# Attention scores from rounded halves of K and Q, SyncE's transfers of the vectors, and an identity built by GpSimd

## The chip, the cores and the metric

One Trainium2 chip, of which one core is used. The metric is the device time of one execution in microseconds. A core has five engines, each with a queue of its own that it executes in order: TensorE (PE, with PEld for its weight loads), VectorE (DVE), ScalarE (ACT), GpSimd (POOL) and SyncE (SP, which here only starts transfers). They wait for one another by semaphores.

## The reference

A transformer block of 512 tokens by 1024: a gated feed-forward network (FFN, inner width 2816), a mixer, a second FFN, and a gated embedding. The mixer adds two branches, a latent attention with 8 heads and an mLSTM with 4 heads. All is fp32. The part that the change touches is the attention:

```python
s = (jnp.einsum('bqhd,bkhd->bhqk', qn, k_nope)
     + jnp.einsum('bqhd,bkd->bhqk', qr, k_rope))
pr = jax.nn.softmax(s.astype(jnp.float32) * scale, axis=-1).astype(v.dtype)
return jnp.einsum('bhqk,bkhd->bqhd', pr, v)
```

## The kernel before

Activations lie feature-major: 8 tiles of 128 features by 512 tokens. Nearly every product is made from rounded halves: an operand a is split into `a_hi` (rounded by ScalarE to the format fp32r, which PE takes in one pass) and `a_lo = a - a_hi` (subtracted by VectorE), and three products hi·hi, hi·lo and lo·hi are added up in a bank of PSUM (`three`, L294 to L296, and `three_tm`, L301 to L303). Weights come in 193 chunks of 128x1024 through a ring of four slots: SyncE loads `w_raw`, ScalarE writes `w_hi` (L317), VectorE `w_lo` (L324), PE uses them and frees the slot.

*The attention loop.* Before it, VectorE writes Q (all 8 heads, 128 feature rows each, `Q_done`) and K (`K_done`, L1302), and ScalarE Vm. Then 32 blocks s (a head and 128 queries) run through all three engines, each with its own written order:
- PE, iteration s: `scores(s)` (L1017), one fp32 product of a 128-column piece of Q with K[:, head, :] (two records in the trace) into bank 2 + s % 3; then four transposes of block s - 4 (L1025), on iterations 12, 20 and 28 a pair output (L1038, 8 fp32 products for two heads), and six rounded products of the attention gate (L294 to L296), which fill PE's time.
- VectorE, iteration s: reduce(s), the row maximum (L1321); `nb(s)`, its scaled negative (L1322); on 12, 20 and 28 two gate copies (`ga_out`, L1308); the reciprocal of the sum of s - 2 (L1331); on 14, 22 and 30 `oT_lo` (L1312), which waits for ScalarE's `oT_hi`; on odd s the copy of the transposes of s - 4 (L1337); on every fourth s one `w_lo` (L324); on s = 6 to 25 one convolution tap of the other branch (L1222 for the first tap of each of four tiles, L1225 for the rest).
- ScalarE, iteration s: exp(s) with its sum (L1526), which waits for `nb(s)` and for the transposes of s - 4; on even s the copy of the transposes of s - 4 (L1532); the scaling of block s - 2 by its reciprocal (L1537, `norm`); on 14, 22 and 30 `oT_hi` (L1517); on every fourth s one `w_hi` (L317).

*The opening.* ScalarE starts 13 transfers of small vectors (`vec_rows`, 96 rows, read as columns after a transpose) and two of biases before its first computation. SyncE loads the first weights, a 128x128 identity from HBM, x in five parts, and further chunks. PE multiplies something of no use while it waits (`warm`), transposes the gains of the first norm, then x tile by tile, between the first products of FFN 1 (`lead_pe`). ScalarE writes `v_hi` (L2037) and the squares of h (L2043), VectorE `v_lo` and h; GpSimd adds the squares up (L560), and PE sums the result over partitions (L423) before the last products of the lead (L579, L580, L585). `lead_pe` is shared with the mixer and the second FFN; the change puts its new lines there under `n == 0`. Then the loop of FFN 1 begins with L294, at 41.

## Time and profile before

| | us |
|---|---|
| three executions | 1217.08, 1217.12, 1220.69; median 1217.12 |
| the profiled execution | 1217.22 |
| its span, first to last instruction | 1215.4 |
| PE busy | 1204.3 (99%) |
| VectorE busy | 645.3 (53%) |
| ScalarE busy | 461.9 (38%) |
| GpSimd busy | 110.7 (9%) |
| mean granted clock of PE | 0.994 |

Times in the rows are microseconds from the start of the span. A matmul's record lasts longer than the step to the next one, since they overlap in the array: the chain's numbers are the steps. "<-" before an engine and a line names what ended an idle time.

### The profile page before, as it was taken

What the parts mean: (1) busy time and instruction counts of PE and PEld (TensorE: products, weight loads), DVE (VectorE), ACT (ScalarE), POOL (GpSimd) and SP (SyncE); (2) the same over time, 40 slices, a digit from 0 to 9 for tenths busy, and PEclk for the clock granted to TensorE, in tenths of its full rate; (3) what the DMA queues carried; (4) which work ended last, traced back from release to release, by engine and by line L of the source; (5) the groups of instructions that cost most, each with busy time, mean ns of one, the idle gap of its engine ahead of it and who ended that gap; (6) DMA issues with size and microseconds to landing.
All of it is one profiled execution on the core that took longest, in us unless ns stands there. A gap on an engine that the chain in (4) does not pass through costs nothing.

```text
span 1215.4 us, 15133 instructions
## 1 busy us (share of the span) xinstructions
PE 1204.3 (99%) x5580; PEld 978.3 (80%) x5580; DVE 645.3 (53%) x1033; ACT 461.9 (38%) x696; POOL 110.7 (9%) x92
## 2 busy tenths in 40 slices
PE   9999999999999999999999999999999999999998
PEld 7788888888888886656887888888888888888887
DVE  6544444462226797765557874674444444222585
ACT  5232223322124627566343633553233232121472
POOL 3000000000003200000112201210000000000254
PEclk9999999999999999999999999999999999999998
DMA  6333333223232341111522133233333333233211
GB/s 205 119 90 102 102 100 90 89 91 114 100 89 48 70 119 53 53 35 35 157 87 70 62 114 119 97 105 94 104 87 97 99 96 104 88 103 95 96 35 70
DMA packets 102512, 111.92 MB, mean 92 GB/s; under 512 B 15326, under 2 KB 92350, under 8 KB 102214
## 3 DMA queue, kind: packets, MB, share of 16 engines
q1 hardware_dynamic: 98016, 109.20, 29.8%
q10 hardware_dynamic: 4454, 2.16, 0.6%
q8 instruction: 26, 0.43, 0.1%
q14 instruction: 16, 0.13, 0.0%
HBM read 108.19 MB, written 3.16 MB: 92 GB/s over the span
## 4 chain that ended last, share of the span: by engine, by line
PE 91%; DVE 3%; ACT 2%; issue 2%; POOL 1%; DMA 0%; DVEq 0%; SPq 0%; ACTq 0%; POOLq 0%
PE bank L294 25%; PE bank L296 24%; PE bank L295 24%; PE bank L585 2%; PE bank L579 2%; PE bank L580 2%; PE bank L301 1%; PE bank L302 1%; PE bank L303 1%; PE bank L1038 1%; PE bank L423 1%; POOL sqacc L560 1%; PE bank L1017 1%; PE bank L1705 1%; PE bank L1148 1%
## 5 line engine op out<-in xcount | busy, mean ns | idle before, releaser
L324 DVE TENSOR_TENSOR w_lo<-w_raw,w_hi 128x1024 fp32r<-128x1024 f32 x193 | 243.0, 1265 | 351.6 <-ACT w_hi L317 348.7
L294 PE MATMUL bank<-v_hi,w_hi 128*128 128x512 f32 x904 | 357.1, 395 | 0.0
L296 PE MATMUL bank<-v_hi,w_lo 128*128 128x512 f32 x904 | 352.5, 390 | 0.0
L295 PE MATMUL bank<-v_lo,w_hi 128*128 128x512 f32 x904 | 352.1, 390 | 0.0
L317 ACT ACTIVATE w_hi<-w_raw 128x1024 fp32r<-128x1024 f32 x193 | 202.1, 1056 | 358.5 <-PE bank L296 354.9
L294 PEld LDWEIGHTS bank<-v_hi,w_hi 128*128 128x128 f32 x904 | 169.9, 188 | 37.9 <-issue 3.5
L296 PEld LDWEIGHTS bank<-v_hi,w_lo 128*128 128x128 f32 x904 | 169.8, 188 | 35.8
L295 PEld LDWEIGHTS bank<-v_lo,w_hi 128*128 128x128 f32 x904 | 170.0, 188 | 33.7
L294 PE MATMUL bank<-prod_hi,w_hi 128*128 (+1 forms) x352 | 137.2, 390 | 0.0
L296 PE MATMUL bank<-prod_hi,w_lo 128*128 (+1 forms) x352 | 137.0, 389 | 0.0
L295 PE MATMUL bank<-prod_lo,w_hi 128*128 (+1 forms) x352 | 137.0, 389 | 0.0
L295 PEld LDWEIGHTS bank<-prod_lo,w_hi 128*128 128x128 f32 x352 | 66.1, 188 | 13.7
L294 PEld LDWEIGHTS bank<-prod_hi,w_hi 128*128 128x128 f32 x352 | 66.1, 188 | 13.6
L296 PEld LDWEIGHTS bank<-prod_hi,w_lo 128*128 128x128 f32 x352 | 66.1, 188 | 13.5
L434 POOL COPY sqacc<-scratch 128x512 f32<-128x512 f32 x4 | 3.7, 924 | 729.5 <-ACT scratch L491 729.5
L776 ACT ACTIVATE prod_hi<-scratch 128x512 f32 (+1 forms) x44 | 27.0, 633 | 110.9 <-DVE scratch L736 110.9
L736 DVE TENSOR_TENSOR scratch<-bank,scratch 128x512 f32<-128x512 f32 x44 | 28.3, 685 | 65.6 <-PE bank L296 65.6
L579 PE MATMUL bank<-v_hi,w_hi 128*128 128x512 f32 x128 | 51.6, 403 | 0.7 <-ACT v_hi L2037 0.4
L580 PE MATMUL bank<-v_hi,w_lo 128*128 128x512 f32 x128 | 50.7, 396 | 0.0
L770 ACT ACTIVATE scratch<-scratch 128x512 f32<-128x512 f32 x44 | 27.1, 633 | 55.5 <-DVE scratch L724 55.5
L560 POOL TENSOR_TENSOR sqacc<-sqacc,scratch 128x512 f32<-128x512 f32 x28 | 41.1, 1466 | 23.6 <-ACT scratch L550 20.7
L585 PE MATMUL bank<-v_lo,w_hi 128*128 128x512 f32 x128 | 37.3, 396 | 0.2
(263 smaller groups left out, 1349.3 us busy)
## 6 DMA issues: line engine op xcount, KB each, us to landing
w_raw<-in_ffn_w_up SPq DMA_DIRECT2D x44, 512.0 KB, 3.7
w_raw<-in_ffn_w_down SPq DMA_DIRECT2D x44, 512.0 KB, 3.4
w_raw<-in_ffn_w_gate SPq DMA_DIRECT2D x43, 512.0 KB, 3.7
w_raw<-in_w_in SPq DMA_DIRECT2D x32, 512.0 KB, 3.7
w_raw<-in_w_out SPq DMA_DIRECT2D x8, 512.0 KB, 3.4
w_raw<-in_ple_w_gate SPq DMA_DIRECT2D x8, 512.0 KB, 3.3
Mb<-m_rows ACTq DMA_DIRECT2D x8, 256.0 KB, 4.5
w_raw<-in_w_branch_mla SPq DMA_DIRECT2D x4, 512.0 KB, 4.0
```

The costliest lines, as they stand in the source:

```text
L294: nc.tensor.matmul(o, whi, a_hi, start=start, stop=False)
L295: nc.tensor.matmul(o, whi, a_lo, start=False, stop=False)
L296: return nc.tensor.matmul(o, wlo, a_hi, start=False, stop=stop)
L317: nc.scalar.activation(w_hi[:, s, :], w_raw[:, s, :], ACT.Copy).then_inc(w_hi_done, 1)
L324: nc.vector.tensor_tensor(w_lo[:, s, :], w_raw[:, s, :], w_hi[:, s, :].bitcast(F32), ALU.subtract).then_inc(w_lo_done, 1)
L560: nc.gpsimd.tensor_tensor(sqacc[:], sqacc[:], scratch[:, m % 4, :], ALU.add).then_inc(b["h_acc"], 1)
L579: nc.tensor.matmul(o[:], whi, v_hi[:, k, :], start=(k == 0), stop=False)
L580: nc.tensor.matmul(o[:], wlo, v_hi[:, k, :], start=False, stop=False)
L585: last = nc.tensor.matmul(B[4 + 2 * (j % 2) + f][:], wv(N + j, c, c + P)[0], v_lo[:, k, :], start=False, stop=(k == KD - 1))
L736: nc.vector.tensor_tensor(scratch[:, 2 + f, :], B[(6 if first else 2) + f][:], scratch[:, f, :], ALU.mult).then_inc(prod_done, 1)
L770: nc.scalar.activation(scratch[:, f, :], scratch[:, f, :], ACT.Silu).then_inc(silu0 if first else silu_done, 1)
L776: nc.scalar.activation(o, scratch[:, 2 + f, :], ACT.Copy).then_inc(phi, 1)
```

## The change

1. *Scores.* K and Q are split like the other operands. ScalarE rounds K of a head (`K_high`, 128x512) and a block's piece of Q (`Q_high`, 128x128) into `K_hi` and `Q_hi`, rings of four; VectorE subtracts (`K_low`, `Q_low`) into the place of K and Q. `scores(s)` is three products. Heads 0 to 3 and blocks 0 to 3 are split before the loop; in iteration s both engines split block s + 4, and in iterations 9, 11, 17 and 19 heads 4 to 7 as well.
2. *Vectors.* ScalarE starts only the transfer of the first norm's gains. The others, with trig, positions and biases, are started by SyncE behind the four first weight chunks (`small_loads`). PE transposes them into bank 0 just before the sum over h, and VectorE copies them after `w_lo` of chunk 3.
3. *Identity.* GpSimd writes it with a memset and an affine select; its transfer is gone. Four of the eight warm products behind the gains go.
4. *Order of the opening.* x comes in four parts of 256 features, the first of them ahead of the second half of the first weight chunk. PE takes x tile 2 between the first two chunk steps and tile 3 behind the second. ScalarE issues the squares of h earlier.

```diff
-    X_PARTS = [(0, 1), (1, 2), (2, 4), (4, 6), (6, 8)]
+    X_PARTS = [(0, 2), (2, 4), (4, 6), (6, 8)]
...
             chunks(0, [0])
+            x_tiles(2, 3)
             chunks(1, [0])
-            x_tiles(2, 4)
+            x_tiles(3, 4)
...
+        if n == 0:
+            pe.wait_ge(consts_in, CONSTS)
+            b.wait(pe, "h_ready", KD)
+            nc.tensor.transpose(B[0][:, 0:NVEC], vec_rows[0:NVEC, :], ident[0:NVEC, 0:NVEC]).then_inc(vecs_T, 1)
         b.wait(pe, "h_acc", KD)
...
             if b == 0:
-                pe.wait_ge(ms["K_done"], hd + 1)
+                pe.wait_ge(ms["qk_split"], QK_COUNT["K", hd])
+            pe.wait_ge(ms["qk_split"], QK_COUNT["Q", s])
...
-            nc.tensor.matmul(B[2 + s % 3][:], Q[:, hd, b * P:(b + 1) * P], K[:, hd, :], start=True,
-                             stop=True).then_inc(ms["scores"], 1)
+            o, q_lo = B[2 + s % 3][:], Q_lo[:, hd, b * P:(b + 1) * P]
+            nc.tensor.matmul(o, Q_hi[:, s % 4, :], K_hi[hd % 4][:], start=True, stop=False)
+            nc.tensor.matmul(o, Q_hi[:, s % 4, :], K_lo[:, hd, :], start=False, stop=False)
+            nc.tensor.matmul(o, q_lo, K_hi[hd % 4][:], start=False, stop=True).then_inc(ms["scores"], 1)
...
+    K_STEP = {9: 4, 11: 5, 17: 6, 19: 7}
...
+    def Q_high(act, s):
+        hd, b = head_block(s)
+        act.wait_ge(ms["Q_done"], HEADS)
+        if s >= 4:
+            act.wait_ge(ms["scores"], s - 3)
+        nc.scalar.activation(Q_hi[:, s % 4, :], Q[:, hd, b * P:(b + 1) * P], ACT.Copy).then_inc(ms["qk_hi"], 1)
...
+    def Q_low(dve, s):
+        hd, b = head_block(s)
+        c = slice(b * P, (b + 1) * P)
+        dve.wait_ge(ms["qk_hi"], QK_COUNT["Q", s])
+        nc.vector.tensor_tensor(Q_lo[:, hd, c], Q[:, hd, c], Q_hi[:, s % 4, :].bitcast(F32),
+                                ALU.subtract).then_inc(ms["qk_split"], 1)
...
             if s % 4 == 1 and s >= 5:
                 lo_upto(dve, GAC + (s - 5) // 4 + 3)
+            if s + 4 < STEPS:
+                Q_low(dve, s + 4)
+            if s in K_STEP:
+                K_low(dve, K_STEP[s])
             if s >= 6 and s - 6 < 4 * CONV:
                 conv_tap(dve, s - 6)
...
             if s >= 14 and s % 8 == 6:
                 oT_high(s // 8 - 1)
+            if s + 4 < STEPS:
+                Q_high(act, s + 4)
+            if s in K_STEP:
+                K_high(act, K_STEP[s])
             if s % 4 == 0 and s >= 4:
                 hi_upto(act, GAC + (s - 4) // 4 + 3)
...
-        sp.dma_start(ident[:], const["ident"]).then_inc(ident_in, 16)
         x_part(0)
+        first_chunk_half_sp(sp, 1)
         x_part(1)
-        first_chunk_half_sp(sp, 1)
+        f1[5](sp, 0, 1)
         x_part(2)
-        f1[5](sp, 0, 1)
         x_part(3)
-        x_part(4)
...
+        f1[0](sp, 2, small_loads)
...
+        plink(pool, nc.gpsimd.memset(ident[:], 0.0))
+        nc.gpsimd.affine_select(out=ident[:], in_=ident[:], compare_op=ALU.not_equal, fill=1.0, base=0,
+                                pattern=[[-1, P]], channel_multiplier=1).then_inc(pool_made, 1)
...
         half_hi(act, 0, 1)
+        x_square(0)
         x_hi(2)
+        x_square(1)
         x_hi(3)
         half_hi(act, 1, 0)
         half_hi(act, 1, 1)
-        x_square(0)
-        x_square(1)
+        x_square(2)
+        x_square(3)
...
-        warm(8, ident[:])
+        warm(4, ident[:])
```

## Rows read from the trace of the kernel before

**Rows 1.** The page: busy time by engine, and the chain's shares by engine

```profile
PE 1204.3 (99%) x5580; PEld 978.3 (80%) x5580; DVE 645.3 (53%) x1033; ACT 461.9 (38%) x696; POOL 110.7 (9%) x92
PE 91%; DVE 3%; ACT 2%; issue 2%; POOL 1%; DMA 0%; DVEq 0%; SPq 0%; ACTq 0%; POOLq 0%
```

**Rows 2.** The chain in order of time, attention loop: start, us, what

```profile
476.86 0.86 PE bank L1017 x2
...
479.55 0.86 PE bank L1017 x2
...
491.59 3.58 PE bank L1038 x16
```

**Rows 3.** Waits from 464 to 568: us in total, times, longest

```profile
ACT Pm L1526 <- DVE small L1322: 25.9, 18, 2.3
DVE small L1321 <- PE bank L1017: 20.8, 12, 4.5
```

**Rows 4.** Timeline of VectorE, blocks 13 to 16: start, us, line, operation, idle before

```profile
499.17 1.21 DVE L324 TENSOR_TENSOR w_lo<-w_raw,w_hi 128x1024 fp32r<-128x1024 f32 x1
...
500.96 0.68 DVE L1321 TENSOR_REDUCE small<-bank 128x1 f32<-128x512 f32 x1
...
504.47 0.69 DVE L1312 TENSOR_TENSOR oT<-bank,oT 128x512 fp32r<-128x512 f32 x1 [2.51 <-ACT oT L1517]
505.08 0.74 DVE L1225 SCALAR_TENSOR_TENSOR mqk<-conv_in,cols,mqk 128x512 f32<-128x512 f32 x1
...
508.83 0.47 DVE L1222 TENSOR_SCALAR mqk<-conv_in,cols 128x512 f32<-128x512 f32 x1
```

**Rows 5.** Timeline of ScalarE, block 14; last, its squares (ns min/median/max)

```profile
501.99 0.78 ACT L1526 ACTIVATE Pm<-bank,small 128x512 f32<-128x512 f32 x1 [1.82 <-DVE small L1322]
502.66 0.19 ACT L1526 ACTIVATION_READ_ACCUMULATOR Pm<-bank,small 128x1 f32 x1
502.75 0.58 ACT L1532 ACTIVATE scratch<-bank 128x512 f32<-128x512 f32 x1
503.23 0.72 ACT L1537 ACTIVATE Pm<-Pm,small 128x512 f32<-128x512 f32 x1
503.85 0.59 ACT L1517 ACTIVATE oT<-bank 128x512 fp32r<-128x512 f32 x1
...
L1606 ACT ACTIVATE scratch<-HS x4: 291/292/294, 686.2 to 687.1; 128x128 f32<-128x128 f32 x4
```

**Rows 6.** Timeline: VectorE's K, reduces 0 and 28, PE's next stage

```profile
455.87 5.71 DVE L1302 TENSOR_TENSOR K<-bank,scratch 64x512 f32<-64x512 f32 x8
...
465.24 0.69 DVE L1321 TENSOR_REDUCE small<-bank 128x1 f32<-128x512 f32 x1 [3.66 <-PE bank L1017]
...
542.25 0.69 DVE L1321 TENSOR_REDUCE small<-bank 128x1 f32<-128x512 f32 x1 [0.53 <-PE bank L1017]
...
567.84 0.50 PE L301 MATMUL bank<-w_hi,v_hi 128*128 128x512 f32 x1
```

**Rows 7.** The chain in order of time, opening

```profile
4.18 3.71 PE bank L2092 x16
...
13.60 0.70 ACT v_hi L2037
...
33.00 0.43 PE bank L579
...
37.45 0.23 PE bank L579
```

**Rows 8.** GpSimd's affine selects on another tile: ns min/median/max, starts

```profile
L1941 POOL TENSOR_SCALAR_AFFINE_SELECT maskbig<-maskbig x2: 287/552/818, 406.8 to 407.6; 128x128 f32<-128x128 f32 x2
```

**Rows 9.** Stretches: us, busy of PE, PEld, DVE, ACT, POOL, granted clock, DMA share, GB/s

```profile
30.00:33.00 3.00, 1.20 (x10) 1.05 (x10) 0.78 (x1) 0.47 (x1) 1.90 (x1) 1.00 0.68 203
33.00:36.50 3.50, 3.50 (x10) 2.72 (x10) 3.08 (x13) 0.00 (x0) 0.00 (x0) 0.51 0.33 116
```

**Rows 10.** Timeline of SyncE: its first load of the FFN loop

```profile
13.02 6.85 SPq L643 DMA_DIRECT2D w_raw<-in_ffn_w_gate  x2
```

## What the change will do to the time

> **What bounds the kernel now.** I read the page's busy table and its chain first: TensorE (PE) is busy for 1204.3 of 1215.4 us and carries 91% of the chain [rows 1]. A change to another engine is therefore worth nothing unless PE waits, and each microsecond that PE is held comes straight onto the end. The change touches two stretches, the attention loop and the first 41 us. For the loop I read the chain in order of time. One block (scores, transposes of an older block, six gate products) takes 479.55 - 476.86 = 2.69 us, of which the fp32 score product takes 0.86, and every eighth block has a pair output of 3.58 on top [rows 2]. A rounded product takes 0.23 at full clock [rows 7]. Then I read the waits. VectorE waited 20.8 us for scores and ScalarE 25.9 us for `nb` from VectorE: both have slack, and it is there because neither of them waits for the other's *present* block beyond `nb` [rows 3]. How tightly they stand all the same I read from their two timelines at block 14 [rows 4, 5].
>
> **Part 1, scores.** Three rounded products of 0.23 replace 0.86: 0.18 less per block, 32 x 0.18 = 5.8 us if PE stays the bound. PE's block becomes 2.51, averaging (28 x 2.51 + 3 x 3.58) / 28 = 2.9 with the pair outputs. The added 32 + 8 roundings on ScalarE and 32 + 8 subtractions on VectorE are short. What decides is where they stand. In block s, VectorE issues `Q_low(s + 4)` after its reduce, `nb`, reciprocal, copies and `w_lo`, and waits there for `Q_high(s + 4)`. ScalarE issues that after exp(s), which waits for `nb(s)` from VectorE in the same block, after the even copy of s - 4, and after the scaling of s - 2. Behind VectorE's wait are queued the convolution tap and the reduce of s + 1, which needed nothing from ScalarE's present block before (only exp(s - 3)). That the split is for a block four later doesn't help: each engine executes in order, so VectorE and ScalarE now take turns once per block. Before has this pattern in blocks 14, 22 and 30, where VectorE waits for `oT_hi` behind exp, copy and scaling: it stood 2.51 us, and the tap and the next reduce started only after it [rows 4].
>
> One turn, start of reduce(s) to start of reduce(s + 1):
> - reduce, `nb`, release of ScalarE: 501.99 - 500.96 = 1.03 [rows 4, 5]
> - exp: 502.75 - 501.99 = 0.76; scaling: 503.85 - 503.23 = 0.62 [rows 5]
> - `Q_high`, 128x128: no row of its own. The nearest are squares of 128x128 at 0.29 and the 512-wide rounding of oT at 0.59 [rows 5]; I take 0.31, and 0.03 to release VectorE (503.85 + 0.59 to 504.47) [rows 4, 5]: 0.34
> - `Q_low`: a VectorE subtraction takes 1.21 for 1024 columns and 0.69 for 512 [rows 4], so about 0.30 for 128; the next one starts 0.08 before an end (504.47 + 0.69 against 505.08): 0.21
>
> Sum 2.96. Even blocks from 4 on add the copy, 503.23 - 502.75 = 0.48 [rows 5]. Blocks 6 to 25 add a tap behind `Q_low`: 0.74 less the 0.08 is 0.66 for 16 of them, 0.47 less 0.09 is 0.38 for the first tap of each of four channel tiles [rows 4]. VectorE's own work in this time (odd blocks: `nb` 0.13, reciprocal 0.07, copy 0.6, every second time `w_lo` 1.1) is no longer than ScalarE's path from `nb` to `Q_high` (about 2.0), so it is covered.
>
> Over the 28 blocks that have such a turn (0 to 27):
> 28 x 2.96 = 82.9; blocks 0 and 1 have no scaling, -1.2; 12 even copies, +5.8; taps 16 x 0.66 + 4 x 0.38 = +12.1; heads 4 to 7 in blocks 9, 11, 17, 19 add `K_high` and `K_low`: `K_low` ends 0.20 + 0.59 + 0.03 + 0.61 = 1.43 after `Q_high` starts, where `Q_low` would end after 0.34 + 0.21, 4 x 0.88 = +3.5; blocks 14 and 22 add `oT_hi` and `oT_lo` in sequence (0.62 + 0.61, less the 0.34 beside it), 2 x 0.89 = +1.8; pair outputs make the next scores some 0.36 late twice, +0.7; the first exp still waits for its table, +0.3. Together 105.9 us. Before, reduce 0 starts at 465.24 and reduce 28 at 542.25: 77.0 us [rows 6]. **So the loop gets 28.9 us longer here**, at 3.8 us a block against PE's 2.9. After reduce 28 nothing couples the two. Before needs 567.84 - 542.25 = 25.6 us from there [rows 6]. I give back 2: 3 x 0.18 for the last scores and about 1.4 because PE, no longer the late one, has begun the last-but-one pair output. Net +27.
>
> The splits before block 0 I cost at nothing: ScalarE has few instructions there, and VectorE, done with K at 455.87 + 5.71 = 461.6, finishes four `K_low` (0.61) and four `Q_low` (0.21), 3.3 us, by 464.9, before the first reduce at 465.24 [rows 6]; scores(0) needs only two heads and one block, by 463.1. That cover is 0.3 us thin; without it the cost is what exceeds it.
>
> Bounds. With `Q_high` at the 0.19 of the shortest ScalarE instruction in rows 5, 0.12 x 28 = 3 us less. At the 0.59 of the 512-wide row, 0.28 x 28 = 8 more. The loop part is +24 to +35.
>
> **Part 2, the opening.** Before, PE fills from 4.18 to 7.89 with eight fp32 warm products (16 records) and only then transposes x [rows 7]. After: four of them, and the identity comes from GpSimd instead of a transfer (nearest row: two affine selects of 128x128 took 0.29 and 0.82 [rows 8]), so x's landing decides. Its first part is now 512 KB, second on SyncE's queue. Anything from 2 us earlier to 1 us later is possible; warm products at half speed follow; I take -0.7. The stop between transposes and v_hi at 13.60 goes, since each pair of chunks has an x tile between them: -0.8 (0.70 of ScalarE and the release) [rows 7]. From 30 on PE waits for GpSimd's sum of squares: busy 1.20 of 3.00 us, 1.8 idle and 2.0 with the pipeline's end, and then a granted clock of 0.51 for 3.5 us [rows 9], in which some nine products take 0.43 instead of 0.23 [rows 7]. After: squares of tiles 0 to 3 are issued some 4 us earlier, h's tile 7 some 2 us, and a vector copy is gone from VectorE before it. The last add then ends near 27, PE arrives near 28: -2.0 for the wait and -1.9 for the clock. Sum -5.4, taken as -5.5.
>
> Moved onto SyncE are 14 transfers, together with two that it had, behind the four first weight chunks: some 6 us of issuing, and the next load (gate, at 13.02) is queued behind them [rows 10]. PE needs that chunk at the end of the opening (41 before, 35 after), so it costs nothing; were it uncovered, 4 to 6 us. PE's wait for all the vectors moves from 17 to 28 us and is covered too. Bounds -8 (x 2 us early) to -1 (GpSimd's sum still last).
>
> **Sum.** The profiled execution took 1217.22 (span 1215.4 and 1.8 around it), the median of three is 1217.12; the difference is nothing. 1217.2 + 27 - 5.5 = **1238.7 us**.
>
> **Rivals.**
> - *PE stays the bound*: the splits are four blocks ahead and the added work is small. For: both engines idle over 20 us for others in this stretch [rows 3], more than the added instructions take (40 x 0.2 and a little). Against: the order in the queues. -5.8 - 5.5 gives 1205.9. It decides if ScalarE's path from `nb` to `Q_high` is under about 1.2 us per block; the rows say 1.7 to 2.2. Chance 0.08.
> - *TensorE's clock falls in the loop*. PE will wait in most blocks, busy about 2.9 of 3.8 us. The one place in the rows where it fell, PE had been busy 1.20 of 3 us [rows 9]; no wait in a turn comes near that. At the lower of its two levels (1.2 GHz; 0.43 a product) a block costs 9 x 0.43 + 0.8 = 4.7, with two pair outputs of 7.2: 28 x 4.7 + 14 = 146 instead of 106, +34 after what overlaps: 1273. Chance 0.04. The Trainium skill has a rule on this side (TensorE: Matmul & The Clock Gate, "A second HAM failure mode: psum-queue depth-cycling"): an engine that idles briefly and often between groups of matmuls, as it cycles through PSUM banks, can go back and forth between the clock levels. By that rule this rival would be likely; the trace has no such stretch, so no run here shows it.
> - *SyncE's burst of small transfers comes late* and PE waits for vectors or the next chunk, then at half clock: the opening gives +1.5 instead of -5.5, 1245.7 with the loop as forecast. It decides if a chunk or the vectors land after PE asks (28 and 35 us). Chance 0.05.
>
> The forecast keeps 0.83. Its own bounds are 1217.2 + 24 - 8 = 1233 and 1217.2 + 35 - 1 = 1251; both ends at once are unlikely, and a term that I missed can be on either side, so the range is **1230 to 1250**. It leaves out the first two rivals. A measurement can tell 0.3% from no change. Slower by more: 0.91; faster: 0.08 (the first rival); within 0.3%: 0.01, a loop that couples half as much and an opening at its best.
>
> **What would show it.** Scores: three products at a pitch of 0.23. In the loop: VectorE idle before `Q_low`, released by ScalarE's `Q_high`, over 30 us in all; PE idle for over 15 us, before the transposes, released by the scaling; reduces 3.0 to 4.6 apart in blocks 6 to 25; clock full. Opening: first gate product at 9 to 10 us, no wait for GpSimd near 30, no products at 0.43 after it, and the first loop of the first FFN (now at 41) at about 35.5. The forecast is wrong if PE is gapless in the loop, or if the reduces stay 2.7 apart.

## The result, and the profile of the changed kernel

The changed kernel takes 1239.99 us (median of four runs, 1238.14 to 1241.18), the kernel before 1217.1 (four runs beside them): a ratio of 1.018, 95% interval 1.017 to 1.020. That is 22.9 us slower, inside the forecast range and 1.3 us over the forecast. The profiled execution took 1240.76 us with a span of 1238.7, 23.3 over the span of before.

The page of after, with the lines that answer to [rows 1], and its line of the granted clock in 40 slices:

```profile
PE 1206.5 (97%) x5604; PEld 985.1 (80%) x5604; DVE 657.7 (53%) x1073; ACT 474.4 (38%) x736; POOL 109.2 (9%) x94
PEclk9999999999998998889999999999999999999998
PE 91%; DVE 4%; ACT 3%; issue 2%; DMA 1%; SPq 0%; DVEq 0%; ACTq 0%
```

PE is busy 2.2 us longer, though its scores are cheaper, and its share falls from 99 to 97%: it now stands idle. The clock is lower in slices 16 to 18 (464 to 557 us), which lie in the attention loop, and in slice 13 (372 to 403 us), the boundary behind the first FFN. VectorE and ScalarE got 12.4 and 12.5 us more work each. That is too little for 23 us at shares of 53 and 38%, unless it lies on a path.

The waits from 460 to 600 us, which answer to [rows 3] (total, times, longest):

```profile
ACT Pm L1588 <- DVE small L1373: 49.3, 31, 2.3
DVE Q_lo L1275 <- ACT Q_hi L1264: 34.9, 20, 2.4
PEld bank L1039 <- ACT Pm L1599: 24.7, 15, 2.7
PE bank L1039 <- ACT Pm L1599: 18.3, 15, 2.3
```

VectorE's wait for ScalarE's `Q_high` is new and 34.9 us long, ScalarE's wait for `nb` has nearly doubled (25.9 before), and VectorE's wait for scores, 20.8 before, is gone from the list's head (2.5 are left). The two engines wait for each other, and PE for both. Block 8 shows one turn. VectorE first, then ScalarE (start, us, operation, idle before):

```profile
485.31 0.68 DVE L1372 TENSOR_REDUCE small<-bank 128x1 f32<-128x512 f32 x1
486.03 0.21 DVE L1373 TENSOR_SCALAR small<-small 128x1 f32<-128x1 f32 x1
486.16 0.15 DVE L1382 RECIPROCAL small<-small 128x1 f32<-128x1 f32 x1
488.53 0.29 DVE L1275 TENSOR_TENSOR Q_lo<-Q,Q_hi 128x128 fp32r<-128x128 f32 x1 [2.22 <-ACT Q_hi L1264]
488.74 0.74 DVE L1239 SCALAR_TENSOR_TENSOR mqk<-conv_in,cols,mqk 128x512 f32<-128x512 f32 x1
489.41 0.68 DVE L1372 TENSOR_REDUCE small<-bank 128x1 f32<-128x512 f32 x1
```

```profile
486.34 0.78 ACT L1588 ACTIVATE Pm<-bank,small 128x512 f32<-128x512 f32 x1 [1.93 <-DVE small L1373]
...
487.11 0.59 ACT L1594 ACTIVATE scratch<-bank 128x512 f32<-128x512 f32 x1
487.59 0.72 ACT L1599 ACTIVATE Pm<-Pm,small 128x512 f32<-128x512 f32 x1
488.20 0.30 ACT L1264 ACTIVATE Q_hi<-Q 128x128 fp32r<-128x128 f32 x1
```

Read them as one line: reduce 485.31, exp 486.34, copy 487.11, scaling 487.59, `Q_high` 488.20, `Q_low` 488.53, tap 488.74, reduce 489.41. Each step starts when the one before it ends. What the other engine does meanwhile (VectorE a reciprocal, ScalarE a `w_hi` behind `Q_high`) is short or off this path. The block takes 489.41 - 485.31 = 4.10 us.

From the starts of the reduces, the loop (reduce 0 to reduce 28) runs from 459.79 to 568.00: 108.2 us against 77.0 in [rows 6]. The whole balance, from landmarks of the two timelines: the products of the h sum at the boundary behind the first FFN begin 6.7 us earlier (370.97 against 377.69), that boundary gives 1.3 back (reduce 0 is 5.45 earlier), the loop adds 31.2, the work behind reduce 28 gives 2.3 back (568.00 to 591.3, before 25.6), and the rest of the kernel is the same to 0.2 us. -6.7 + 1.3 + 31.2 - 2.3 = 23.5, against 23.3 in the spans.

Then the clock in the loop. Stretches of after, columns as in [rows 9]:

```profile
459.80:480.00 20.20, 15.97 (x64) 12.15 (x62) 10.64 (x28) 12.66 (x28) 0.00 (x0) 0.83 0.12 32
480.00:500.00 20.00, 12.51 (x59) 8.99 (x60) 12.52 (x30) 11.15 (x26) 0.00 (x0) 0.92 0.15 48
500.00:520.00 20.00, 18.84 (x84) 12.39 (x83) 12.81 (x30) 10.49 (x23) 0.00 (x0) 0.91 0.09 27
520.00:540.00 20.00, 14.12 (x56) 7.82 (x55) 12.89 (x31) 10.87 (x24) 0.00 (x0) 0.83 0.09 27
540.00:560.00 20.00, 17.44 (x87) 13.53 (x85) 12.83 (x31) 12.10 (x27) 0.00 (x0) 1.00 0.09 27
```

The forecast said a full clock here. PE's clock goes to its lower level (1.2 GHz) for parts of the loop, in a pattern of waits of which the longest was 2.3 us before a matmul and 2.7 before a weight load. The Trainium skill has a rule that the prediction had quoted as unproven here (TensorE: Matmul & The Clock Gate, "A second HAM failure mode: psum-queue depth-cycling"): frequent short idle times between groups of matmuls, in a kernel that cycles through PSUM banks, can make the clock go back and forth. These rows agree with it. The chain of after shows where it lands on the path, the pair output of block 12, 5.64 us where [rows 2] have 3.58:

```profile
499.77 5.64 PE bank L1052 x16
...
505.92 0.71 ACT Pm L1599
506.64 0.21 ACT Q_hi L1264
```

The opening. PE's timeline of after, its first products, and further on the products of the h sum:

```profile
3.19 2.08 PE L2164 MATMUL bank<-ident 128*128 128x128 f32 x8
5.27 1.15 PE L2182 MATMUL bank<-ident,x_tm 128*128 128x128 f32 x8
6.25 1.06 PE L2164 MATMUL bank<-ident 128*128 128x128 f32 x8
7.07 0.47 PE L583 MATMUL bank<-v_hi,w_hi 128*128 128x512 f32 x1
...
26.90 0.97 PE L427 MATMUL bank<-ones,sqacc 128*128 128x1 f32 x8
27.74 0.48 PE L583 MATMUL bank<-v_hi,w_hi 128*128 128x512 f32 x1
...
34.10 0.48 PE L298 MATMUL bank<-v_hi,w_hi 128*128 128x512 f32 x1
```

The first gate product is at 7.07 us, not at the 9 to 10 that I forecast; the h sum finds GpSimd's result ready (its last add ends at 25.4), and no half clock follows.

### The profile page after: what moved, and what is told of

Same layout as the page of the kernel before. It is cut to its first block, busy times and chain, and to the rows that moved or that the text cites. A ratio compares the mean times of both kernels' runs of the same rounds, so it can differ in the third digit from the quotient of the medians.

```text
span 1238.7 us, 15320 instructions
## 1 busy us (share of the span) xinstructions
PE 1206.5 (97%) x5604; PEld 985.1 (80%) x5604; DVE 657.7 (53%) x1073; ACT 474.4 (38%) x736; POOL 109.2 (9%) x94
## 4 chain that ended last, share of the span: by engine, by line
PE 91%; DVE 4%; ACT 3%; issue 2%; DMA 1%; SPq 0%; DVEq 0%; ACTq 0%
PE bank L298 24%; PE bank L300 24%; PE bank L299 24%; PE bank L589 2%; PE bank L583 2%; PE bank L584 2%; PE bank L1052 1%; PE bank L305 1%; PE bank L306 1%; PE bank L307 1%; PE bank L427 1%; ACT Pm L1599 1%; PE bank L1039 1%; DVE small L1372 1%; PE bank L1771 1%
## 5 line engine op out<-in xcount | busy, mean ns | idle before, releaser
L299 PE MATMUL bank<-v_lo,w_hi 128*128 128x512 f32 x904 | 352.3, 390 | 0.0
L1588 ACT ACTIVATE Pm<-bank,small 128x512 f32<-128x512 f32 x32 | 24.9, 778 | 49.3 <-DVE small L1373 49.3
```

What stands on the lines that cost most here:

```text
L299: nc.tensor.matmul(o, whi, a_lo, start=False, stop=False)
L1588: nc.scalar.activation(Pm[:, q, :], B[2 + s % 3][:], ACT.Exp, bias=nb[:, q:q + 1], scale=rqs[:, b:b + 1], accum_out=sums[:, s:s + 1]).then ...
```

## Experiments

Beside the time, each is read by the same three numbers: start of reduce 0, length of the loop (reduce 0 to 28), and the way from reduce 28 to the next stage. These come from the timelines of the profiled executions, in us. The ratios compare with executions of before in the same job, whose median was 1217.1 for after, 1217.3 for e1 to e4, 1218.0 for e6 and e10, and 1217.0 for e11:

| kernel | median | against before in the same job | reduce 0 | loop | reduce 28 to the next stage |
|---|---|---|---|---|---|
| before | 1217.3 | | 465.24 | 77.0 | 25.6 |
| after | 1240.0 | 1.018 (1.017 to 1.020) | 459.79 | 108.2 | 23.3 |
| e1 opening only | 1210.3 | 0.996 (0.994 to 0.998) | 458.25 | 77.0 | 25.6 |
| e2 scores only | 1246.5 | 1.024 (1.022 to 1.027) | 466.06 | 108.3 | 23.3 |
| e3 rounding first | 1213.0 | 0.997 (0.996 to 0.998) | 457.61 | 79.7 | 24.7 |
| e11 subtraction later | 1213.7 | 0.997 (0.995 to 0.998) | 457.59 | 79.5 | 24.7 |
| e4 work, no link | 1222.0 | 1.004 (1.002 to 1.005) | 465.39 | 79.2 | 25.5 |
| e10 splits on GpSimd | 1208.5 | 0.993 (0.990 to 0.995) | 457.67 | 75.2 | 25.6 |
| e6 idle products | 1241.1 | 1.020 (1.018 to 1.022) | 457.27 | 108.3 | 23.3 |
| e5 one more, ScalarE | 1246.1 (one) | | 457.57 | 115.2 | 24.4 |
| e5b one more, VectorE | 1243.6 (one) | | 458.65 | 111.1 | 24.9 |

Single executions of one program differ by some 4 us (20 runs of before: 1213.99 to 1218.28), so a term of 1 or 2 us is read from the traces' landmarks and not from the times. My theory: the loss is the link, VectorE's wait in a block for ScalarE's work of the same block. The main rival: it is the amount of work that was added.

### Each part alone

`e1_opening_only` is the changed kernel with the scores of before:

```diff
-            nc.tensor.matmul(o, Q_hi[:, s % 4, :], K_hi[hd % 4][:], start=True, stop=False)
-            nc.tensor.matmul(o, Q_hi[:, s % 4, :], K_lo[:, hd, :], start=False, stop=False)
-            nc.tensor.matmul(o, q_lo, K_hi[hd % 4][:], start=False, stop=True).then_inc(ms["scores"], 1)
+            nc.tensor.matmul(B[2 + s % 3][:], Q[:, hd, b * P:(b + 1) * P], K[:, hd, :], start=True,
+                             stop=True).then_inc(ms["scores"], 1)
...
-            if s + 4 < STEPS:
-                Q_low(dve, s + 4)
...
-            if s + 4 < STEPS:
-                Q_high(act, s + 4)
```

> The changed kernel's opening (vectors' transfers by SyncE, identity on GpSimd, new order of x tiles and squares) with the fp32 scores of before. If the two parts of the change add up: the first loop of the first FFN starts at 34.3 us as in the changed kernel (41.1 before), the boundary behind the first FFN loses 1.4 us again, reduces 0 to 28 of the attention loop take 77.0 us as before, and the time is 5.3 to 6 us under before, about 1211.5. If the gain of the opening hung on the other loop (it is not there, or given back elsewhere): within 1 us of 1217.

Measured: -7.0 us by the medians, the loop at 77.02 as before, first FFN's boundary 7.0 us earlier. The gain is there in full and independent of the loop; it is 1.5 us more than I forecast for it, and more than the 5.3 to 6 expected for this run: I had expected the next boundary to take 1.4 us back, as in after, and here it does not (87.5 us from its h sum to reduce 0, as in before).

`e2_scores_only` is the reverse, the kernel before with `K_high`, `Q_high`, `K_low`, `Q_low` and the three products.

> The split scores with the opening of before (two pairs of semaphores are shared, since the pool is full). If the whole of the loss is in the attention loop: reduces 0 to 28 take 108 us, the clock in it falls to between 0.83 and 0.92 in stretches of 20 us, and the time is 27 to 29.5 us above before, about 1245.5. If the loss comes in part from how the shifted opening meets the loop (its phase against the weight transfers): under +24.

Measured: +29.2 us and a loop of 108.26 us. Its 31 distances between reduces agree with those of after to 0.02 us, though it meets them 6.3 us later. The loop doesn't depend on the opening, and the parts add: -7.0 + 29.2 = +22.2, measured +22.9.

### The link or the work

`e3_high_first` moves two calls in ScalarE's block; no instruction is added or taken away:

```diff
         for s in range(STEPS + 4):
+            if s + 4 < STEPS:
+                Q_high(act, s + 4)
+            if s in K_STEP:
+                K_high(act, K_STEP[s])
...
-            if s + 4 < STEPS:
-                Q_high(act, s + 4)
-            if s in K_STEP:
-                K_high(act, K_STEP[s])
```

> The changed kernel with one move: ScalarE issues Q_high(s + 4) and K_high at the head of block s, before it waits for nb(s), for the transposes of s - 4 and for the scaling of s - 2. All instructions are the same. Theory 1 (place in the queue): VectorE's Q_low finds its operand ready, its waits for Q_high fall from 34.9 us to under 5, VectorE no longer takes turns with ScalarE, PE is the bound again at 2.5 us a block, reduces 0 to 28 take 72 to 75 us, and the time is about 1206 (1204 to 1210), under both kernels. Theory 2 (amount of work: 80 more instructions fill ScalarE and VectorE): no work is taken away, so 1236 to 1241. In between, such as 1215 to 1225, a second coupling would be next, and VectorE's or ScalarE's waits name it.

Measured: 1213.0 us, loop 79.7. Waits of this kernel from 460 to 565:

```profile
ACT Pm L1592 <- DVE small L1373: 21.9, 19, 2.3
...
PEld bank L1039 <- ACT Pm L1603: 10.2, 11, 1.5
DVE small L1372 <- PE bank L1032: 8.1, 4, 4.0
...
DVE Q_lo L1275 <- ACT Q_hi L1264: 2.2, 4, 0.8
```

The wait for `Q_high` is 2.2 us instead of 34.9, and 28.5 us of the loop went with it. Theory 2 has fallen. But the time isn't the 1206 of theory 1: the loop is 5 to 8 us over the 72 to 75 that I expected.

`e11_low_next` breaks the same link from the other side, on VectorE, which leaves the rounding at the end of ScalarE's block:

```diff
-            if s + 4 < STEPS:
-                Q_low(dve, s + 4)
-            if s in K_STEP:
-                K_low(dve, K_STEP[s])
+            if 1 <= s and s + 3 < STEPS:
+                Q_low(dve, s + 3)
+            if s - 1 in K_STEP:
+                K_low(dve, K_STEP[s - 1])
```

> The changed kernel with one move on VectorE alone: in block s it subtracts Q_low(s + 3), whose rounding ScalarE issued at the end of block s - 1, in place of Q_low(s + 4), whose rounding stands at the end of ScalarE's present block; K_low comes one block later as well. ScalarE's order is that of the changed kernel. Theory 1 (VectorE's wait for ScalarE's present block is the cost): the operand is there, VectorE's waits for Q_high fall from 34.9 us to under 5, reduces 0 to 28 take 77 to 82 us, as with the rounding at the head of ScalarE's block (79.7), time 1209 to 1215. Theory 2 (ScalarE's rounding at the end of its block holds back the next exp, and its place there is the cost): the loop stays over 95 us and the time over 1225.

Measured: 1213.7 us, loop 79.5, and the wait for `Q_high` is no longer among the first eight. It is the same result by another move, so neither engine's place alone is the cause. The cause is that producer and consumer stand in the same block.

`e4_work_only` is the kernel before with the added work and no link:

```diff
+            if s + 4 < STEPS:
+                nc.vector.tensor_tensor(junk_d[:, s % 4, :], v_hi[:, 0, 0:P].bitcast(F32), v_hi[:, 1, 0:P].bitcast(F32), ALU.subtract)
...
+            if s + 4 < STEPS:
+                nc.scalar.activation(junk_a[:, s % 4, :], v_hi[:, 0, 0:P].bitcast(F32), ACT.Copy)
```

> Before, with fp32 scores, and the added work alone in the places of the loop where the change has it: in blocks 0 to 27 one 128x128 rounding on ScalarE at the block's end and one 128x128 subtraction on VectorE before the tap, both on constant data into tiles that nobody reads, and no wait between the two engines. Theory 1 (only the link between the queues costs): before plus 0 to 2 us, reduces 0 to 28 at 77 to 79 us. Theory 2 (the work itself costs): 28 times 0.3 to 0.6 on the path, +8 to +17 us, or with the full effect +29.

Measured: 4.7 us over before, a miss for theory 1's 0 to 2, and far from theory 2's 8 to 17. The loop is 79.2, 2.2 us over before and just over theory 1's range, so a pair of unlinked instructions costs 0.08 us on average, where a linked pair costs 1.1 (31.2 / 28, with the four splits of K, which this run left out). The other 2.6 us of the 4.7 are not in the loop. They lie at the last boundary, where this execution had a granted clock of 0.74 in 1142 to 1155 and the one of before 1.00.

### What is left when the link is gone

In e3 PE is busy 73.3 of 79.7 us in the loop, so it isn't PE that is late. ScalarE is, in the first blocks. Stretches of before (blocks 0 to 7), then of e3 (blocks 0 to 7), columns as in [rows 9]:

```profile
465.24:480.44 15.20, 14.64 (x58) 8.90 (x57) 11.79 (x28) 13.03 (x26) 0.00 (x0) 1.00 0.25 70
```

```profile
457.61:473.96 16.35, 14.03 (x70) 10.79 (x69) 13.48 (x36) 14.53 (x35) 0.00 (x0) 1.00 0.22 65
```

ScalarE was busy 13.0 of 15.2 us there already before; with 1.5 us more it is busy 14.5 of 16.35, and I put down to it the 1.15 us by which these blocks grew. That is argued from the shares; the next run tests it. My "PE stays the bound" rival had this wrong as well: it credited 5.8 us for the scores although the weight load ahead of the transposes waited 6.8 us for the scaling already in before.

`e10_splits_pool` gives the loop's splits to GpSimd, which did nothing there:

```diff
+        pool.wait_ge(ms["qk_split"], 8)
+        for s in range(STEPS):
+            if s + 4 < STEPS:
...
+                pool.wait_ge(ms["scores"], s + 1)
+                nc.gpsimd.tensor_copy(Q_hi[:, s % 4, :], Q[:, hd, c]).then_inc(ms["qk_hi"], 1)
+                pool.wait_ge(ms["qk_hi"], QK_COUNT["Q", s + 4])
+                nc.gpsimd.tensor_tensor(Q_lo[:, hd, c], Q[:, hd, c], Q_hi[:, s % 4, :].bitcast(F32), ALU.subtract).then_inc(ms["qk_split"], 1)
...
```

The lines left out do the same for K of heads 4 to 7, and take the loop's splits away from ScalarE and VectorE.

> The changed kernel with the roundings and subtractions of the loop (Q from block 4, K from head 4) on GpSimd, which has nothing to do there, four blocks ahead as before; ScalarE and VectorE then execute in blocks 0 to 31 what they executed before the change. The run with the roundings at the head of ScalarE's block has a loop (reduce 0 to 28) of 79.7 us, of which PE is busy 73.3, and the run with the work alone and no link lost 2.2 us. Theory 1 (what is left there is the added work on two nearly full engines): the loop falls to 72 to 76 us and the time to 1203 to 1208. Theory 2 (PE's waits for the scaling are a chain of reduce, exp and scaling that is no shorter when scores are): the loop is at 76 to 78 us, as before the change, and the time at 1208 to 1212. Theory 3 (GpSimd's work slows VectorE's): taps longer than 0.74 us and a loop over 79 us.

Measured: 1208.5 us, loop 75.2, the shortest loop of all and a kernel 0.75% under before (the time would fit theory 2, but the profiled execution had a granted clock of 0.86 in 1120 to 1140, at the last boundary, where before had 1.00; I go by the loop). Theory 1 holds there: with no added work on ScalarE and VectorE it is 4.5 us shorter than e3's. Yet of the 5.0 us (28 x 0.18) that cheaper scores could bring, 1.8 arrive. Theory 2 has a part in it too: that weight load still waits 6.8 us for the scaling, as in before. Theory 3 is there, and small. The costliest groups of e10 in the loop (busy, mean ns, idle before):

```profile
L1239 DVE SCALAR_TENSOR_TENSOR mqk<-conv_in,cols,mqk 128x512 f32<-128x512 f32 x16 | 13.3, 829 | 0.0
...
L1711 POOL TENSOR_TENSOR Q_lo<-Q,Q_hi 128x128 fp32r<-128x128 f32 x28 | 15.2, 541 | 2.2
L1236 DVE TENSOR_SCALAR mqk<-conv_in,cols 128x512 f32<-128x512 f32 x4 | 2.8, 693 | 0.0
```

A two-operand tap takes 829 ns on average against 739 in before, and the first tap of a channel tile, a `tensor_scalar`, 693 against 473: 16 x 0.09 + 4 x 0.22 = 2.3 us of VectorE. The averages hide where it is. 13 of the 16 two-operand taps took 0.73 to 0.75, as in before, though several of them ran beside GpSimd's 128x128 work. Four taps carry 2.2 of the 2.3 us, and each overlaps with one of GpSimd's four 128x512 subtractions for a head of K (1.29 to 2.38 us each): they took 1.78, 1.10, 0.68 and 1.08 us. The longest of them:

```profile
477.52 1.78 DVE L1239 SCALAR_TENSOR_TENSOR mqk<-conv_in,cols,mqk 128x512 f32<-128x512 f32 x1
```

GpSimd's cast of 128x128 took from 0.28 up to 0.78 us. The Trainium skill says that the two engines share their way into the SBUF, with contention where VectorE's instruction has two SBUF inputs or is in a 2-port mode (GPSIMD Engine Reference, "1. Specifications", the row on SBUF interfaces). The trace agrees for the splits of K, and shows next to no cost for those of Q. So the 128x512 subtractions are what to keep off GpSimd here; I didn't run that.

### Does a turn really add up?

`e5_one_more` puts one 128x64 rounding ahead of `Q_high` on ScalarE, `e5b_one_more_vector` one 128x64 subtraction ahead of `Q_low` on VectorE, each in blocks 0 to 27 and in the changed kernel:

```diff
             if s + 4 < STEPS:
+                alink(act, nc.scalar.activation(extra[:], v_hi[:, 0, 0:64].bitcast(F32), ACT.Copy))
                 Q_high(act, s + 4)
```

```diff
             if s + 4 < STEPS:
+                dlink(dve, nc.vector.tensor_tensor(extra[:], v_hi[:, 0, 0:64].bitcast(F32), v_hi[:, 1, 0:64].bitcast(F32), ALU.subtract))
                 Q_low(dve, s + 4)
```

> The changed kernel with one more instruction on ScalarE in each of blocks 0 to 27, a 128x64 rounding of constant data into a tile that nobody reads, ahead of Q_high(s + 4), which waits for its end. Turn theory: it lies on the path from nb to Q_high in every block, so its duration and link, 0.3 to 0.4 us, come 28 times: the loop grows from 108.2 to 116.5 to 119.5 us, span +8 to +11. If the loop were bound by something else (PE's clock, VectorE's work): under +3.

> The changed kernel with one more instruction on VectorE in each of blocks 0 to 27, a 128x64 subtraction of constant data into a tile that nobody reads, with a link to its end, right before the wait for Q_high(s + 4). Turn theory: VectorE stands idle there for 0.5 to 2.3 us, so it costs nothing, but in the few blocks where w_lo fills VectorE's time up to Q_high: loop 108.2 to 110 us. If VectorE's work were what counts: 28 times 0.25 to 0.35, +7 to +10.

Measured: on ScalarE +7.0 us in the loop, on VectorE +2.9. ScalarE's timeline of e5, block 8:

```profile
487.41 0.72 ACT L1600 ACTIVATE Pm<-Pm,small 128x512 f32<-128x512 f32 x1
488.02 0.25 ACT L1604 ACTIVATE extra<-v_hi 128x64 fp32r<-128x64 f32 x1
488.30 0.31 ACT L1265 ACTIVATE Q_hi<-Q 128x128 fp32r<-128x128 f32 x1
```

The instruction and its link take 488.30 - 488.02 = 0.28 us, and most blocks are longer by 0.27 to 0.31 (0.29 in block 8, 0.28 in block 27); of the blocks with a pair output, 12 grew by 0.74 and 20 got shorter by 0.40. 28 x 0.28 = 7.8, of which 7.0 arrive, under the 8 to 11 expected: I had the instruction too long, and blocks 5, 14 and 22, where VectorE is the later one of the two, did not grow at all. On VectorE those three grew by 0.26 each (block 5 with its two `w_lo`, blocks 14 and 22 behind `oT_lo`), 0.8 in all. 17 blocks grew by 0.06 to 0.08, 1.2 in all, although VectorE has long ended the extra instruction there. In block 8 it lies between the two engines: from the start of `Q_high` to that of `Q_low` it is 487.82 to 488.22, 0.40 us, against 0.33 in after. In blocks 9, 11, 17 and 19, where a head's split follows, nothing of it is left (0.01 or less). Why the hand-over is longer I leave open. The other 0.9 are in blocks 12, 13, 21 and 25, around the pair outputs. So my 0 to 1.8 was exceeded. The two answers tell the path from the rest: an instruction on ScalarE between `nb` and `Q_high` costs all of itself, one on VectorE's waiting side about a third.

### The lower clock in the loop

`e6_keep_warm` has PE execute idle products while it would wait:

```diff
-            pe.wait_ge(ms["norm"], t + 1)
             if t >= 2:
                 pe.wait_ge(ms["pt_even"] if t % 2 == 0 else ms["pt_odd"], t // 2)
+            if 1 <= t < 24:
+                for _ in range(5):
+                    nc.tensor.matmul(B[5 + t % 2][:, 0:P], ident[:], ident[:], start=True, stop=True)
+            pe.wait_ge(ms["norm"], t + 1)
```

> The changed kernel, and in blocks 1 to 23 PE executes five 128x128 fp32 products on the identity, into a free bank, ahead of its wait for the scaling (these fill some 1.1 us of an idle time of up to 2.3). If the reduced clock (0.83 to 0.92 in stretches of 20 us) costs on the path only where the even copy waits for the pair output: pair outputs at 3.58 again instead of 5.64, blocks 12 and 20 at 4.1 to 4.5 us instead of 5.4 and 5.0, the loop 1.5 to 2.5 us shorter than 108.2, the time 1237.5 to 1238.5. If the clock costs nothing in the loop: within 0.5 us of 1240. If the idle products hold the transposes up: 1241 to 1245.

Measured: 1241.1 us, which can't be told from after (ratios to before 1.020 and 1.018, with intervals that overlap), and a loop of 108.3. Of the three outcomes the first and the third both came, and cancel. The clock did come back. Stretch of e6:

```profile
500.00:520.00 20.00, 18.86 (x119) 16.05 (x115) 12.31 (x29) 10.93 (x24) 0.00 (x0) 1.00 0.09 27
```

Block 12 took 4.64 instead of 5.44 and block 20 took 4.60 instead of 5.04, -1.24 (a little over the 4.1 to 4.5 expected). But blocks 13, 21 and 22 took 0.55, 0.54 and 0.24 more, +1.33: the idle products stood in front of transposes for which somebody waited. No other block differs from after by more than 0.02. So the lower clock costs 1.2 us of the loop. While VectorE and ScalarE take turns, PE has time even at half clock, and only the pair outputs show it.

### Where the opening's 7 us come from

Three runs take back one part each of e1; one execution each, read by their landmarks. A caution first: seven other kernels (after, e3, e5, e5b, e6, e10, e11) have the opening of e1, instruction for instruction, and their profiled executions spread. Their first gate product comes at 6.70 to 8.73, GpSimd's last add ends at 25.4 to 26.8, and the boundary behind FFN 1 is at 371.0 to 372.4. A difference of 1 to 1.5 us in one execution is therefore not shown by the landmark alone.

| kernel | x transposes | first gate product | GpSimd's last add ends | h sum's products | boundary behind FFN 1 |
|---|---|---|---|---|---|
| before | 7.68 | 10.12 | 31.9 | 31.9 | 377.7 |
| e1 | 5.24 | 7.43 | 25.2 | 26.7 | 370.7 |
| e7 eight warm products | 6.71 | 8.40 | 26.2 | 27.6 | 371.7 |
| e8 vectors by ScalarE | 5.12 | 8.81 | 26.6 | 28.1 | 372.1 |
| e9 squares late | 5.06 | 7.65 | 28.7 | 28.7 | 374.5 |

```diff
-        warm(4, ident[:])
+        warm(8, ident[:])
```

> The changed opening with the scores of before, and eight warm products instead of four ahead of the transposes of x. Theory 1 (the first product came 3 us earlier because PE's warm products, not x, held the transposes of x: 16 records up to 7.68 before, 8 up to 5.27 after): the transposes start at 7.0 to 7.4 instead of 5.25, the first gate product at 8.8 to 9.3 instead of 7.43, and the first loop of the first FFN about 0.5 to 2 us later than 34.3. Theory 2 (x's landing decides, and lands earlier because the identity's transfer is gone from the head of SyncE's queue): the transposes stay at 5.3.

```diff
-            for name, rows in VEC_ROWS[1:]:
-                sp.dma_start(vec_rows[VEC[name]:VEC[name] + rows, :], vec_src(name)).then_inc(consts_in, 16)
...
+        for name, rows in VEC_ROWS[1:]:
+            act.dma_start(vec_rows[VEC[name]:VEC[name] + rows, :], vec_src(name)).then_inc(consts_in, 16)
...
```

> The changed opening with the scores of before, and 14 small transfers (vectors and biases) issued by ScalarE again, ahead of its first rounding. If their place on ScalarE's queue costs: ScalarE starts its first roundings of x or of weights later, first product over 7.7 us (7.43 without), squares and GpSimd's last add later by as much. If not: first product 7.1 to 7.6, the last add ends at 25 to 26 us, the span within 1 us of 1207.8, and the part of the change that moved them to SyncE is worth nothing.

```diff
-        x_square(0)
         x_hi(2)
-        x_square(1)
         x_hi(3)
...
-        x_square(2)
-        x_square(3)
+        x_square(0)
+        x_square(1)
...
```

> The changed opening with the scores of before, and ScalarE's instructions in the order of before (squares 0 and 1 behind the first six roundings, 2 and 3 behind a group of weight roundings). If the order of the squares is what took PE's wait for GpSimd away: GpSimd's last add ends 1.5 to 4 us later than 25.2, at 27 to 29; the products of the h sum, at 26.7 now, follow it, and where PE stands idle for over 1 us there, a reduced clock behind it: span +1 to +4 on 1207.8. If the earlier first product is what did it: the last add ends by 26.5 and the span is within 1 us of 1207.8.

e7: the transposes start 1.5 us later, at 6.71 (7.0 to 7.4 expected), where the eight kernels with four warm products start them at 4.95 to 5.41, so x had landed and the warm products had held it. The later landmarks move by 1.0, which is within the spread. The transfers that e8 gives back to ScalarE are a term that I had not seen at all: of the two outcomes in its expectation the first one came. ScalarE's timeline of e8, then of e1:

```profile
1.78 0.36 ACTq L2076 DMA_DIRECT2D vec_rows<-in_mix_pre_norm  x1
...
6.98 0.37 ACTq L2078 DMA_DIRECT2D small<-in_ml_f_bias  x1
7.40 0.63 ACT L344 ACTIVATE w_hi<-w_raw 128x512 fp32r<-128x512 f32 x1 [4.51 <-issue]
```

```profile
3.52 0.63 ACT L344 ACTIVATE w_hi<-w_raw 128x512 fp32r<-128x512 f32 x1 [0.64 <-DMA w_raw<-in_ffn_w_gate]
```

The 14 issues stand in ScalarE's queue from 1.47 to 7.35 us, and the first weight rounding comes at 7.40 instead of 3.52; PE then has its x and waits for the weight's low half. e8 is 1.4 us later than e1 at each later landmark. The late rounding is shown by these rows; the 1.4 is within the spread, so its size is an estimate. e9 is the largest, and clear of the spread: GpSimd's last add ends at 28.7 instead of 25.2, PE's h sum waits for it, and the clock falls behind that as in [rows 9] (stretch of e9):

```profile
28.00:34.00 6.00, 5.27 (x21) 4.31 (x22) 4.85 (x15) 0.05 (x1) 0.67 (x1) 0.73 0.52 159
```

It costs 3.8 us at the next boundary (374.5, against 370.7 in e1 and 372.4 in the latest of the others), and 4.7 us of the span, over the 1 to 4 expected. Together 1.0 + 1.4 + 3.8 = 6.2 of 7.0, of which the 3.8 is shown and the others are rough. What the x tile between each pair of chunks, the four parts of x and the identity built by GpSimd are worth I didn't run alone.

## Why the prediction was right, and where it was off

- **The mechanism of the loop** is as forecast: the two queues take turns, and the link makes them do it (e3, e11, e4).
- **The turn.** Forecast 2.96 for an odd block without a tap, 3.44 for an even one, 3.62 and 4.10 with a tap, 0.88 more with a head's split. Blocks 27, 26, 7, 8 and 9 of after took 2.95, 3.43, 3.61, 4.10 and 4.53 (3.61 + 0.92). `Q_high`, for which I had no row, took 0.30 and 0.33 to `Q_low` (488.20 to 488.53), against 0.31 and 0.34.
- **The loop's sum**, 105.9 forecast, 108.2 measured. Two terms account for it. I wrote that VectorE's own work up to `Q_low` is always covered, with one `w_lo` in the count; block 5 has two of them, 2.35 us, and took 3.98 instead of 2.96: +1.0. And I gave the pair outputs 0.36 late twice at full clock; blocks 12 and 20 took 5.44 and 5.04 instead of 4.10: +2.3 where the sum has +0.7. By e6, 1.2 of the 2.3 is the clock; at full clock the two blocks were 0.54 and 0.50 late, so the 0.36 was short as well. That leaves -0.3 for all else.
- **The clock.** The forecast said full, and gave its rival 0.04. The clock fell in 4 of 5 stretches of the loop. My ground was that no wait was as long as the one in [rows 9]. The rows of after show the lower level behind waits of 1 to 2.7 us too. That the number held all the same is luck: the price was wrong too, in the other direction. I priced a half-clock loop at +34, as if PE were then the bound, and e6 puts it at 1.2, because the products run at half speed where PE would otherwise wait.
- **Behind reduce 28**: -2 forecast, -2.3 measured.
- **The opening**, -5.5 forecast, -6.7 in after and -7.0 in e1. The first product was to come 0.7 earlier and came 3.05 earlier, beyond my own bound of 2: I let x's landing decide, where warm products (e7) and ScalarE's issues (e8) did, by some 1.0 and 1.4. The half clock and GpSimd's sum, -3.9 forecast, are 3.8 in e9. What is left of the opening I did not run.
- **The sum.** In the spans the misses are +2.3 (loop), -1.2 (opening), +1.3 (the boundary below) and -0.3 (behind reduce 28). That the time fits to 1.3 us owes something to their signs.
- **What was to show it.** The waits were as said: VectorE 34.9 us for `Q_high` (over 30), PE 18.3 us for the scaling (over 15). But I had said reduces 3.0 to 4.6 apart in blocks 6 to 25. Four blocks are over it: 12 and 20, and 14 and 22 with 4.99 and 4.98, which my own terms for `oT_hi` and `oT_lo` put at 4.99; the sign was written too narrow.
- **The splits before block 0**, put at nothing: from the first gate product behind the first FFN's boundary to scores(0) it is 75.9 us in before and in after, so they cost nothing.
- **What I didn't have**: the boundary behind the first FFN, where the change adds and removes no instruction in the first 12 us. From its h sum to reduce 0 it is 87.5 us in before, e1 and e4, 88.8 in after and e2, 86.3 in e3, e5, e5b, e6, e10 and e11. The difference arises in those 12 us, by the clock. In the stretch from 4 to 8 us behind it the granted clock was 0.63 in before and 0.50 in after, and in the next 4 us 1.00 and 0.76; in e3 it was 1.00 in both. In after the eight broadcasts of `L420` took 1.91 us, at the lower clock level, against 1.06 in before. What sets the clock there stays open:

```profile
374.75 4.19 PE L461 MATMUL bank<-ident 128*128 128x128 f32 x18
378.73 1.91 PE L420 MATMUL bank<-ident,small 128*128 128x128 f32 x8
```

- **SyncE's burst** cost nothing, as said: the loads behind it were in time and the first FFN's loop starts at 34.10 without a wait.

## What to carry to other kernels

A result that is needed four blocks later is still needed now if its producer and its consumer stand in the same turn of two in-order queues: write down who is queued behind each new wait, and put at least one block between the two. A link like that puts the work of both engines in one line, here 31 us for 28 pairs that cost 2 us unlinked; moving the two calls took 28.5 us of it back. What an engine that is hardly used could take over (here GpSimd) is the next thing to look for, before cheaper arithmetic on an engine that already waits. And count the transfers that an engine issues as its work: 14 of them stood in ScalarE's queue for 5.9 us at the start, and its first rounding came 3.9 us later.

## What the runs showed of the hardware that I had not expected

- TensorE's clock fell to its lower level for parts of the loop though no wait in it was over 2.7 us, and was at its upper level in e6, with five 128x128 products in each wait (0.91 in after and 1.00 in e6, in 500 to 520). It cost 1.2 us of 108, since PE was not the late one.
- The clock at the boundaries between stages isn't the same in programs whose instructions there are the same: the way from the first one to reduce 0 came out at 86.3, 87.5 or 88.8 us with a granted clock of 1.00, 0.63 or 0.50 in the same four microseconds, and at the last one the clock was 1.00 in before and 0.74 in e4. This moves a time by 1 to 3 us, as much as many edits are worth.
- VectorE's instructions beside GpSimd's 128x512 subtractions took longer: two-operand taps of 128x512 1.78 and 1.08 instead of 0.74 us, one-operand ones 1.10 and 0.68 instead of 0.47. Beside GpSimd's 128x128 work nearly all took what they took in before. GpSimd's own 128x128 cast took between 0.28 and 0.78 us.
- The same opening, in the profiled executions of eight kernels, had its first gate product at 6.70 to 8.73 us and reached the boundary behind the first FFN at 370.7 to 372.4.
